# Two experts' tokens picked by one group of matmuls, in the branch for at most 128 tokens each

## The reference

```python
def moe_swiglu(h, w_router, b_router, w1, w3, w2):
    t = h.reshape(-1, shp[-1])                       # 256 tokens x 1024
    logits = (t @ w_router).astype(f32) + b_router
    top_v, top_i = lax.top_k(logits, TOP_K)          # TOP_K = 2, N_EXPERTS = 8
    top_w = jax.nn.softmax(top_v, axis=-1)
    combine = sum(one_hot(top_i, N_EXPERTS) * top_w[..., None], axis=1)
    for e in range(N_EXPERTS):                       # FFN_DIM = 2816
        y += combine[:, e:e + 1] * ((silu(t @ w1[e]) * (t @ w3[e])) @ w2[e])
```

## Time and profile before

| what | value |
|---|---|
| time, median of 3 runs | 2524.56 us (2521.57 to 2525.34) |
| span of the profiled execution | 2522.7 us |
| expert stage, first weight matmul to last spread | 1004.9 to 1809.8 us of it |
| TensorE matmuls, share of the span | 98% |
| VectorE, ScalarE | 72%, 52% |
| DMA, mean over the span | 202 GB/s |
| granted TensorE clock, mean | 0.983 |

### The profile page before, as it was taken

One profiled execution on the slowest core, in us unless ns is written; L12 is line 12 of the kernel. 1 busy time (PEld: TensorE's weight loads), 2 busy tenths in 40 slices (PEclk: granted clock), 3 DMA queues, 4 the chain that ended last, 5 costly groups with the idle time before them and its releaser, 6 DMA issues.

```text
span 2522.7 us, 33560 instructions
## 1 busy us (share of the span) xinstructions
PE 2460.3 (98%) x13301; PEld 1992.0 (79%) x13301; DVE 1816.5 (72%) x2875; ACT 1312.4 (52%) x1992; POOL 66.4 (3%) x71
## 2 busy tenths in 40 slices
PE   7999999999999988999999999999999999999998
PEld 2565648788786767888888888888798999989998
DVE  6788627676432454999999999999777775676774
ACT  3135513222232453877778777777645554545553
POOL 0000010000010000000000000000000000000000
PEclk9999999999999999999999999999899999999999
DMA  7522023555412102989889889898743445433442
GB/s 291 224 99 92 1 84 150 197 201 185 149 67 84 51 17 102 354 334 364 332 332 364 336 334 364 332 367 333 266 168 118 151 181 198 157 134 133 168 184 101
DMA packets 71653, 510.71 MB, mean 202 GB/s; under 512 B 7905, under 2 KB 9057, under 8 KB 10049
## 3 DMA queue, kind: packets, MB, share of 16 engines
q1 hardware_dynamic: 68690, 500.21, 52.1%
q10 hardware_dynamic: 2208, 6.32, 0.7%
q0 software_dynamic: 592, 1.97, 0.2%
HBM read 506.23 MB, written 2.23 MB: 202 GB/s over the span
## 4 chain that ended last, share of the span: by engine, by line
PE 86%; DVE 8%; ACT 4%; issue 1%; DMA 1%; POOL 0%; ACTq 0%; DVEq 0%
PE bank L816 84%; DVE UL L2087 2%; ACT UH L1604 1%; DVE arena L2095 1%; PE bank L1188 1%; DMA consts<-in_c 1%; ACT arena L1607 1%; DVE XT L2095 1%; PE bank L931 1%; ACT XT L1607 0%; DVE arena L2787 0%; DVE HT L2087 0%; DVE arena L2091 0%; DVE small L2154 0%; ACT arena L1831 0%
## 5 line engine op out<-in xcount | busy, mean ns | idle before, releaser
L2087 DVE TENSOR_TENSOR UL<-ring,UH 128x1024 fp32r<-128x1024 f32 (+1 forms) x804 | 970.0, 1218 | 320.8 <-ACT UH L1604 301.0
L1604 ACT CAST UH<-ring 128x1024 fp32r<-128x1024 f32 (+1 forms) x804 | 830.3, 1040 | 560.7 <-PE bank L816 531.2
L816 PE MATMUL bank<-XH,UH 128*128 128x256 f32 x1040 | 302.2, 291 | 4.5 <-DVE UL L2087 3.4
L816 PE MATMUL bank<-XL,UH 128*128 128x256 f32 x1040 | 294.0, 283 | 0.0
L816 PE MATMUL bank<-XH,UL 128*128 128x256 f32 x1040 | 293.9, 283 | 0.0
L816 PE MATMUL bank<-UH,HGh 128*128 128x512 f32 (+1 forms) x768 | 290.5, 378 | 3.4 <-issue 2.3
L816 PE MATMUL bank<-UH,HGl 128*128 128x512 f32 (+1 forms) x768 | 287.4, 374 | 0.0
L816 PE MATMUL bank<-UL,HGh 128*128 128x512 f32 (+1 forms) x768 | 286.7, 373 | 0.0
L2134 DVE CUSTOM_DVE_ANT_0 JUNK<-ring,CROW 128x1024 bf16<-128x1024 f32 x176 | 206.3, 1218 | 13.1 <-ACT CROW L1607 9.9
L816 PE MATMUL bank<-arena 128*64 128x256 f32 (+7 forms) x856 | 197.5, 372 | 13.8 <-ACT arena L1604 4.6
L816 PEld LDWEIGHTS bank<-XH,UH 128*128 128x128 f32 x1040 | 198.8, 191 | 14.4 <-issue 6.7
(11 more groups left out here) (217 smaller groups left out, 4017.0 us busy)
## 6 DMA issues: line engine op xcount, KB each, us to landing
ring<-in_w SPq DMA_DIRECT2D x477, 1024.0 KB, 4.9
XT<-in_x ACTq DMA_DIRECT2D x2, 1024.0 KB, 11.4
bias_scratch<-BIAS POOLq DMA_DIRECT2D x6, 192.0 KB, 2.1
consts<-in_c ACTq DMA_DIRECT2D x1, 1109.0 KB, 7.9
out_y<-XT ACTq DMA_DIRECT2D x2, 512.0 KB, 3.5
BIAS<-bias_scratch POOLq DMA_DIRECT2D x1, 768.0 KB, 7.1
constd<-in_c ACTq DMA_DIRECT2D x1, 768.0 KB, 4.3
consts<-in_c ACTq DMA_DIRECT2D x1, 512.0 KB, 17.0
```

Source lines behind the costliest of these rows:

```text
L816: return e.matmul(out, lhsT, rhs, start=start, stop=stop, skip_group_check=True)
L1604: return e.copy(out, in_)
L2087: return e.tensor_tensor(out, a, b, op)
```

## The change

In the narrow branch an expert fills at most 128 of the 256 columns of PK. The change puts the one-hots of experts 1 and 2, 3 and 4, 5 and 6 side by side in these columns, so that one pick of 32 matmuls gathers the tokens of both: the first expert in columns 0 to 127 of HGh and HGl, the second in 128 to 255. `couple` names the experts of a pick, `lead` the first of them, `slot0` the first column. At the joint before experts 2, 4 and 6 there is no pick; `order` is rotated as if there were. Expert 7 is picked alone, over 128 columns. Expert 0's pick is as before. For the counts to stay equal, a pick for two signals eight times, and ScalarE and VectorE copy its four banks in eight halves of 256 columns; SC is made in two halves of 128 columns. The wide branch computes what it did. `Signal` now keeps its values by branch. In the diff the first `picked` is ScalarE's, `one_hot` and the second `picked` are VectorE's.

```diff
+        def lead(e_, wide):
+            return e_ if wide or e_ % 2 or not e_ else e_ - 1
+
+        def couple(e_, wide):
+            return [e_] if wide or not e_ or e_ == 7 else [e_, e_ + 1]
+
+        def slot0(e_, sbk, wide):
+            return 128 * (sbk if wide else e_ - lead(e_, wide))
...
-            def pick(e_):
+            def pick(e_, wide=True):
+                es = couple(e_, wide)
+                if not wide and lead(e_, wide) != e_:
+                    order.extend(order[:5])
+                    del order[:5]
+                    return
+                n = 256 if wide or len(es) == 2 else 128
                 bs = [take(w, ("pick", e_, i)) for i in range(4)]
                 w.wait_ge(*vec.at("pk", e_))
                 w.wait_ge(*vec.at("htok", 1, 1))
                 for d in range(8):
-                    dst = bs[d // 2][:, 256 * (d % 2):256 * (d % 2) + 256]
+                    dst = bs[d // 2][:, 256 * (d % 2):256 * (d % 2) + n]
                     for tb in range(2):
-                        mm(dst, HTh[:, tb, 128 * d:128 * d + 128], PK[:, tb, :], tb == 0, False)
+                        mm(dst, HTh[:, tb, 128 * d:128 * d + 128], PK[:, tb, 0:n], tb == 0, False)
...
-                        i = mm(dst, low, PK[:, tb, :], False, tb == 1)
-                    if d % 2:
+                        i = mm(dst, low, PK[:, tb, 0:n], False, tb == 1)
+                    if len(es) == 2:
+                        i.then_inc(*sums.up(("pick", e_, d // 2)))
+                    elif d % 2:
                         i.then_inc(*sums.up(("pick", e_, d // 2)))
...
-                for sbk in range(2):
+                for sbk in range(n // 128):
                     for tb in range(2):
-                        i = mm(b[:, 2 * sbk:2 * sbk + 2], PK[:, tb, 128 * sbk:128 * sbk + 128].bitcast(F32), TW[:, tb, e_, :],
-                               tb == 0, tb == 1)
+                        i = mm(b[:, 2 * sbk:2 * sbk + 2], PK[:, tb, 128 * sbk:128 * sbk + 128].bitcast(F32),
+                               TW[:, tb, es[sbk % len(es)], :], tb == 0, tb == 1)
...
-                    w.wait_ge(*vec.at("hg", e_, 3))
+                    w.wait_ge(*vec.at("hg", lead(e_, wide), 3))
                 for sbk in ((1, 0) if wide else (0,)):
...
-                    p = slice(128 * sbk, 128 * sbk + 128)
+                    p0 = slot0(e_, sbk, wide)
+                    p = slice(p0, p0 + 128)
...
+            def picked(e_, wide=True):
+                es = couple(e_, wide)
+                if not wide and lead(e_, wide) != e_:
+                    return
+                if len(es) == 2:
+                    for d in range(8):
+                        w.wait_ge(*sums.at("pick", e_, d // 2))
+                        copy(HGh[:, d, :], psum(("pick", e_, d // 2))[:, 256 * (d % 2):256 * (d % 2) + 256]).then_inc(
+                            *act.up(("hgh", e_, d // 2)))
+                    w.wait_ge(*sums.at("chosen", e_))
+                    for g in es:
+                        copy(SI[:, g, 0, :], psum(("chosen", e_))[:, 2 * (g - e_):2 * (g - e_) + 2]).then_inc(
+                            *act.up(("si", g), free=[("chosen", e_)]))
+                    return
...
+            def one_hot(e_, wide=True):
...
                 for tb in range(2):
-                    ts(PK[:, tb, :], con("iota"), pos[:, tb, e_:e_ + 1], None, ALU.is_equal).then_inc(*vec.up(("pk", e_)))
+                    for g in es:
+                        ts(PK[:, tb, 128 * (g - e_):128 * (g - e_) + n], con("iota", 0, n), pos[:, tb, g:g + 1], None,
+                           ALU.is_equal).then_inc(*vec.up(("pk", e_)))
...
+            def picked(e_, wide=True): 
...
+                if len(es) == 2:
+                    for d in range(8):
+                        w.wait_ge(*act.at("hgh", e_, d // 2))
+                        tt(HGl[:, d, :], psum(("pick", e_, d // 2))[:, 256 * (d % 2):256 * (d % 2) + 256],
+                           HGh[:, d, :].bitcast(F32), ALU.subtract).then_inc(
+                            *vec.up(("hg", e_, d // 2), free=[("pick", e_, d // 2)]))
+                    return
...
-                        for sbk in range(2):
-                            ts(SC[:, sbk, :], con("iota"), SI[:, e_, sbk, 1:2], None, ALU.is_equal).then_inc(
-                                *vec.up(("sc", e_)))
-                        if e_ < 7:
-                            one_hot(e_ + 1)
+                        if wide:
...
+                        else:
+                            for hf in (0, 128):
+                                ts(SC[:, 0, hf:hf + 128], con("iota", hf, 128), SI[:, e_, 0, 1:2], None,
+                                   ALU.is_equal).then_inc(*vec.up(("sc", e_)))
+                        if e_ < 7 and lead(e_ + 1, wide) == e_ + 1:
+                            one_hot(e_ + 1, wide)
```

More of the change, by code:

```diff
@@ L159, in note, with has @@
         for k in keys:
-            self.value[k] = self.n
+            self.value[self.branch, k] = self.n
+    def has(self, *key):
+        return any((b, key) in self.value for b in (self.branch, None, False))
     def at(self, *key):
         if self.known:
-            return self.sem, self.value[key]
+            return self.sem, next(self.value[b, key] for b in (self.branch, None, False) if (b, key) in self.value)
         return self.sem, 0
@@ L529, in build @@
         lo_ready = Signal(sem("weights_low"))
+        signals_all = (sums, vec, act, pool, hi_ready, lo_ready)
         s_ring = [sem(f"ring_loaded{i}") for i in range(RING)]
@@ L778, in cleared @@
             for signal in (vec, act):
[L779 removed]
+                if signal.has("free", prior[tile]):
                     w.wait_ge(*signal.at("free", prior[tile]))
@@ L796, in two_ways @@
             held = list(order), dict(bank), dict(holder)
+            for s in signals_all:
+                s.branch = True
             with e.If(wide):
                 body(True)
-            w.seen = seen
+            then, ends = w.seen, [s.n for s in signals]
+            for s in signals_all:
+                s.branch = False
+            w.seen = dict(seen)
             done[:] = begun
             order[:] = held[0]
-            for now, then in ((bank, held[1]), (holder, held[2])):
+            for now, kept in ((bank, held[1]), (holder, held[2])):
                 now.clear()
-                now.update(then)
+                now.update(kept)
             for s, n in zip(signals, counts):
@@ L808, in two_ways @@
                 body(False)
+            assert ends == [s.n for s in signals]
+            w.seen = {k: min(v, then.get(k, 0)) for k, v in w.seen.items()}
+            for s in signals_all:
+                s.branch = None
         def tensor_program(e):
@@ L1240, in sized @@
                     elif kind == "pick":
-                        pick(e_)
+                        pick(e_, wide)
                     elif kind == "spread":
@@ L1769, in halves @@
                 return fn(0)
-            def picked(e_):
+            def picked(e_, wide=True):
[12 more added lines that the diff above has]
+                    return
+                n = 256 if wide else 128
                 for i in range(4):
                     w.wait_ge(*sums.at("pick", e_, i))
-                    copy(HGh[:, 2 * i:2 * i + 2, :], psum(("pick", e_, i))[:, :].rearrange("p (d n) -> p d n", d=2)
+                    copy(HGh[:, 2 * i:2 * i + 2, 0:n], psum(("pick", e_, i))[:, :].rearrange("p (d n) -> p d n", d=2)[:, :, 0:n]
                          ).then_inc(*act.up(("hgh", e_, i)))
-                evict(("chosen", e_), SI[:, e_, :, :], psum(("chosen", e_))[:, 0:4].rearrange("p (s c) -> p s c", s=2),
-                      ("si", e_))
+                evict(("chosen", e_), SI[:, e_, 0:n // 128, :],
+                      psum(("chosen", e_))[:, 0:n // 64].rearrange("p (s c) -> p s c", c=2), ("si", e_))
             def sized(part, wide):
@@ L1812, in sized @@
                     elif kind == "pick":
-                        picked(e_)
+                        picked(e_, wide)
             def attend2(l, i):
@@ L2431, in halves @@
                 return fn(0)
-            def one_hot(e_):
+            def one_hot(e_, wide=True):
+                es = couple(e_, wide)
                 w.wait_ge(*vec.at("pos"))
                 if e_:
-                    w.wait_ge(*sums.at("chosen", e_ - 1))
+                    w.wait_ge(*sums.at("chosen", lead(e_ - 1, wide)))
+                n = 256 if wide else 128
                 for tb in range(2):
-                    ts(PK[:, tb, :], con("iota"), pos[:, tb, e_:e_ + 1], None, ALU.is_equal).then_inc(*vec.up(("pk", e_)))
-            def picked(e_):
+                    for g in es:
+                        ts(PK[:, tb, 128 * (g - e_):128 * (g - e_) + n], con("iota", 0, n), pos[:, tb, g:g + 1], None,
+                           ALU.is_equal).then_inc(*vec.up(("pk", e_)))
+            def picked(e_, wide=True):
```

(12 more changed lines are left out.)

12 lines of the change are left out of this document (8 added, 4 removed).

## The result

The changed kernel takes 2528.07 us (median of 20 runs, 2519.41 to 2532.24), the kernel before 2521.38 us (20 runs, 2517.26 to 2530.6). The ratio is 1.0020, 95% interval 1.0011 to 1.0028: slower by 2.8 to 7 us, about 5 (the medians differ by 6.7). Forecast were +1.4 us and "same" in a range of 2520 to 2532; the time lies in the range, and the movement is at the edge of what I called no change, on the slow side, nearer to rival B's +6.8 than to my +1.4.

The account below looks back on a forecast made before the run. The expert stage was taken as bound by the tensor engine, with a second ScalarE and VectorE chain nearly as long as the pick. Terms +0.9 - 0.6 + 1.1 = +1.4 us gave 2526.0 us, range 2520 to 2532.

Parts of the forecast that it names:

- rival B: Joints after experts 1, 3, 5: each pause costs two low-clock stretches, 3.1 us each; +6.8 us in all, 2531.4 us; chance 0.15.
- The wait in place of the pick: Joints after experts 1, 3, 5: spread waits for VectorE's low halves, so 0.65 us gained, not 4.59; engine idles 3.9 us.
- The fourth weight unit: Experts 1 to 6: VectorE is no longer late with this unit, the 0.46 step goes, 0.34 us gained at each joint.
- The clock: Joints after experts 1, 3, 5: granted clock falls to 0.50 after the pause, costing 1.3 us each (0 to 3.1).
- my case: Joints without a pick: one low stretch of 3.4 us, partly spent idle; net +0.3 us per joint; chance 0.58.
- rival A: Joints after experts 1, 3, 5: no fall of the clock after the pause; -2.5 us in all, 2522.1 us; chance 0.20.
- the row of 2.30 us: Earlier profile: 2.30 us idle before expert 0's first weight matmul, followed by no clock fall; by it a pause costs 0.
- The pick for two: Joints before experts 1, 3, 5: eight subtractions end 0.15 us later, the late fourth unit's 0.34 goes; -0.2 us each.
- Expert 7: Joint before expert 7, pick alone over 128 columns: between -0.65 and +2.8 us by the unknown step; middle taken, +1.1 us.

Follow-up runs that it names:

- filled kernel: Changed kernel plus 22 unread bf16 matmuls of 384 columns filling the three pauses at joints without a pick: 2517.20 us, ratio 0.9972 to the kernel before.
- its repetition: The changed kernel run again with no edit, beside the kernel before: 2527.88 us against 2522.68, ratio 1.0017.
- the filling before the branch: Changed kernel plus 18 filling matmuls between expert 0's pick and the branch: 2527.95 us against 2521.66 of the kernel before, ratio 1.0019.
- the two with a filling there: Fillings before the branch: in the changed kernel, 2527.95 us; in a version with spread after three next-expert weight units, also filled after expert 7, 2512.81 us.
- single picks: No pairing, against the kernel before: experts 1 to 7 each picked alone over 128 columns; 2515.08 us, ratio 0.9964; again 2514.65 us, ratio 0.9970.

## Why the prediction was right, and where its sizes were off

*The wait in place of the pick.* Right in place and size: spread 0.66 us earlier (0.65), idle of 3.77 us (some 3.6 forecast) put down to VectorE's low halves, the same at all three joints.

*The fourth weight unit.* Right: the slow step is gone at all six joints. With the clock out of the way, these two terms make 0.87 per joint (filled kernel) where I had 0.99. (The half microsecond that I read out of the earlier trace rows is 1.05 - 0.67 = 0.38; no term used it.)

*The clock.* The mechanism was right, the term was mis-sized. I took 1.3 us per joint, from one stretch of 3.4 us that begins before the pause ends. In the nine joints of three profiled executions with the full pause, a stretch followed each time, six times of 3.4 us and three times of 6.8. Experts 2, 4 and 6 took 101.55 us on average, against 99.72 filled: the fall costs 1.8 us. The six stretches of 3.4 us began 4.4 to 5.7 us behind the last down matmul, after the pause of 4.16 had ended, so they lay wholly in busy time and cost 1.5 us (101.25); that they would begin inside it was my error. The three of 6.8 began inside it and cost 2.4 (102.14). The net of such a joint is +1.0 us against before, not +0.3. I had written that the forecast is wrong if the clock stays low for more than one stretch: this was so at two of the three joints of the first profile and at three of the nine. So the joints are a mixture of my case and rival B, whose price of 3.1 was too high; rival A is out for the full pause. The Trainium skill's rule ("TensorE: Matmul & The Clock Gate", section "Why this matters for your kernels"), that pauses of some microseconds bring back half clock, agrees with these nine joints better than the row of 2.30 us that I held against it.

*The pick for two.* -0.2 us forecast; experts 1, 3 and 5 take 100.54 us on average in the profiles of the changed kernel, its repetition, the filled pauses and the filling before the branch (expert 5 of the first, with its late weights, left out), 100.71 before: -0.2.

*Expert 7.* I took the middle of two ends, +1.1 us; measured is the fast end, -0.65 at the spread and 0.4 to 0.7 less for the whole interval, although the step is 0.11 and not 0.06. The Trainium skill's 81 ns per load and matmul at 128 columns (same page, section "Back-to-back issue gap") is not met by this format: 111 ns in this trace.

*What I did not see.* The pause at the branch before expert 0 grew from 2.30 to between 2.76 and 3.00 us in the paired kernels without a filling there, and expert 0 took 1.5 to 1.8 us more in all but the two with a filling there. I had written that nothing moves elsewhere. It is not shown that the change causes it: only one execution of before is profiled, and one of the two with single picks has the low stretch too.

Sum by the profiles: 3 x 1.0 - 3 x 0.2 - 0.6 = +1.8, with expert 0 about +3.4. The measured ratio says +2.8 to +7, which holds the +3.4; low stretches elsewhere, which shift from execution to execution by 5 us and more, hide the rest. That my +1.4 came so near was in part luck: the term of expert 7 was 1.7 us too high, and this hid most of the 2.1 by which the three joints were too low; expert 0 was not in the sum at all.

## What to carry to other kernels

Before matmuls are removed, look for the other chain that ends at the same point; where it is nearly as long as they are, their removal buys only the difference. A pause of a few microseconds in a dense stream costs a second time through the clock, so the freed time must be filled with useful work: here three weight units of the next expert, which turned +5 us into -15. And where two chains end together, narrower instructions at every joint may bring more than fewer at some.

## What the runs showed of the hardware

Idle of 3.77 us before the spread was followed by a low clock nine times in nine, some 2.4 us (2.34 to 2.40) two times in three, 1.97 us not once in three. At the branch, without filling, 2.76 to 3.00 us were followed by a low clock nine times in nine, 2.30 and 2.75 us were not. A 128-column matmul of the kernel's rounded 4-byte format steps by 0.11 us with a load of its own, a 256-column one by 0.118: half the columns save 6%. Entering the branch costs TensorE 2.3 to 3.0 us of idle, and work put before it does not cover all of that: 1.38 us stay idle behind 18 filling matmuls.
